# A transformer layer pair in float32 on one core: first selection, router, context keys and embedding products reordered at the start of the experts

## The chip, the cores and the metric

The kernel runs on one core of a Trainium2 chip. The metric is the device time of one execution, in microseconds (us). The runs shown have a median of 1193.95 us (three runs, 1192.86 to 1196.66). All data are float32.

## The reference, cut to what matters

Two blocks run one after the other on 256 tokens of width 1024. The first mixes (a gated linear recurrence and an attention), then adds a mixture of experts, then adds embeddings' rows times a gate. The second block (convolution, neighbourhood attention with context keys and values from `ctx_2`) follows.

```python
hm = rmsnorm(x, ln_moe[layer]).reshape(B * S, D)
x = x + hierarchical_moe(hm, ...)          # top-1 of 8 groups, then top-2 of its 8 experts
# per expert: (silu(x @ w1[e]) * (x @ w3[e])) @ w2[e], w1 and w3 1024x256, w2 256x1024
ple_gate = jax.nn.sigmoid(rmsnorm(x, ln_ple[layer]) @ w_ple_gate[layer])
x = x + (p[layer] @ w_ple_proj[layer]) * ple_gate
...
kv_c = hc @ w_in[i][:, K_OFF:V_END]        # context keys and values of the second block
```

Each of the 64 experts has three matrices of 1 MB, 192 in all, and every one of them is fetched from HBM.

## The kernel before, in words

All instructions stand in an order written out by hand, one stream for each engine, and engines meet on semaphores. TensorE (`pe`) multiplies, ScalarE (`act`) and VectorE (`dve`) empty its eight banks `B[0..7]`, and SyncE (`sp`) issues nearly all weight loads, in one order, each a DMA of 1 MB. A load for a place that is still in use waits on SyncE, and all later loads wait behind it.

**Stage A** ends with the product `out`, seven submatrix products (L820). Its result is `HN`, the residual. Then follow on TensorE, from L1071 to L1109: two of eight steps `k` of the context keys `kc` (one weight slot, two output halves `parts`, eight steps `k` each), the turning of `HN` (L1084), the other six steps of part 0 of `kc`, the router product (L1093, 8 steps `k` for each half of the tokens, operand `RHT`, which VectorE turns out at L1889 and ScalarE at L1358), part 1 of `kc`, five small products that rank the tokens within their group (L1100 to L1104, they need the group choice `GOH` of VectorE), and three of the four products `pp` of the embeddings (L802 here). `gather(0)` (L1121) needs the selection `SELR`, which VectorE computes in `select_chunk` (L2268). The fourth `pp` stands behind it. `moe_round(0)` follows.

VectorE's order there: logits (L2230), group choice (L2238 to L2245), the experts' logits in that group (L2248, L2250), choice of two experts (`first_max` twice, to L2254), then the rank (L2256 on), `select_chunk`, the tables, and only after the weights `WT` the `sorted_chunk(0)` (L2306), which writes the first gathered rows to `XGS`.

**The experts** run in rounds, one group of eight experts a round and up to 64 tokens; this input has eight rounds. In a round there are four pairs of experts `p`. `up(p)` (L1146) multiplies by `w1` and `w3` of both experts at once: one matmul has 64 stationary columns and streams 512 columns, 256 of `w1` and 256 of `w3`; the two experts use the two halves of the array's columns. `down(p)` (L1187) multiplies by `w2`. The order is up(0), up(1), down(0), up(2), down(1), [gather], up(3), down(2), down(3), then the scatter (L1225).

**Places for weights.** Round 0 has 24 loads. The first 20 have places of their own (`FIRST_PLACES`; B2, B1, B0, R0, VL, R1, R2, X, CK, R3 with two halves each), and are issued during stage A as memory comes free. R3 is the ring's last two slots: its half 0 holds `kc`'s weights before, its half 1 `w_ple_proj`'s. Every later load waits with `moe_used` until the earlier user of its place is done (`before`). A pair of loads of `up` counts as done together, when the whole of `up(p)` is done for that expert. The next loads are, in order: loads 20 to 23 of round 0 (places B2 and B1, free after up(0)); loads 0 to 3 of round 1 (B0 and R0, free after up(1)); loads 4 to 7 of round 1 (R1 and R2, free after up(2)); and so on. L687 issues a `w2`, L691 a `w1` or `w3`.

Of the kernel before, what the change touches and what calls it, by code (L numbers as in the profile page):

```python
# [21 lines left out]
P = 128  # L22
# [97 lines left out]
def build(nc, a, out):  # L120
    with ExitStack() as ctx:
# [113 lines left out]
        PTR = area(9728, 2, T)  # L235
# [15 lines left out]
        XGS = sb("XGS", [P, DK, T + SLOT])  # L251
        RS = sb("RS", [P, 16], I32)
# [185 lines left out]
        for i, n in zip(of["pp"], (0, 1, 3, 2)):  # L438
            bank_no[i] = n
# [108 lines left out]
        for _n in range(SET * UNITS):  # L548
            _r, _u = divmod(_n, UNITS)
            _down = moe_order[2 * _u][0] == "down"  # L550
            if _n < len(FIRST_PLACES):
                _p = FIRST_PLACES[_n]
            elif _r < BIG:
                _p = min((n, p) for p, (n, _) in last_use.items()
                         if (_down or p != "VL") and _n < GONE.get(p, SET * UNITS))[1]
            else:
                _p = RING_PLACES[_u % len(RING_PLACES)]
            past = last_use.get(_p)
            turn = past[1] + 1 if past else 1
            for _h in range(2):  # L560
                place_of[_r, 2 * _u + _h] = (_p, _h)
                turn_of[_r, 2 * _u + _h] = turn
                if past:
                    _q, _v = divmod(past[0], UNITS)
                    up = moe_order[2 * _v][0] == "up"
                    before[_r, 2 * _u + _h] = _q * NM + 2 * _v + (2 if up else 1 + _h)
            last_use[_p] = (_n, turn)
# [73 lines left out]
        def _(sp):  # L641
# [54 lines left out]
            for p, h in (("R0", 0), ("B1", 0), ("B0", 0), ("R0", 1), ("R1", 0), ("R1", 1), ("R2", 0), ("R2", 1), ("X", 0), ("X", 1),  # L696
                         ("CK", 0), ("CK", 1), ("R3", 0), ("VL", 1), ("R3", 1)):
# [14 lines left out]
            for j in range(2 * len(FIRST_PLACES), NM):  # L712
                sp.wait_ge(S("moe_used"), before[0, j])
                expert_dma(j, 0, 0)
# [11 lines left out]
            for r in range(1, SET):  # L726
                g = sp.value_load(RT[0:1, r + 1:r + 2], min_val=0, max_val=NG - 1)
                for j in range(NM):
                    sp.wait_ge(S("moe_used"), before[r, j])
                    expert_dma(j, r, g)  # L730
                    if (r, j) in ctx_behind:
# [37 lines left out]
        def _(pe):  # L769
# [317 lines left out]
            product(of["kc"][0], HT, parts=(0,), ks=range(2, DK))  # L1087
            pe.wait_ge(S("rT_dve"), 4)
            pe.wait_ge(S("rT_act"), 4)
            pe.wait_ge(S("small_in"), SMALL)  # L1090
            for t in range(TT):
                for k in range(DK):
                    mm = pe.matmul(B[4][:, t * 72:t * 72 + 72], RHT[:, k, t * P:t * P + P], RW[:, k, :],  # L1093
                                   start=(k == 0), stop=(k == DK - 1))
            mm.then_inc(S("logits_ps"), 1)
            product(of["kc"][0], HT, parts=(1,))
# [8 lines left out]
            pe.wait_ge(S("p_in"), 16)  # L1105
            for i in of["pp"][:-1]:
                product(i, PTR)


# [16 lines left out]
            def moe_round(r, first=False):  # L1126
# [3 lines left out]
                def up(p, halfway=None):  # L1130
# [4 lines left out]
                    js = [moe_index[("up", 2 * p + e, 0)] for e in range(2)]  # L1135
                    for j in js:
                        slot_in(j, r)
                        slot_in(j + 1, r)
                    for k in range(DK):
                        if k == DK // 2 and halfway is not None:  # L1140
                            turn_hidden(halfway)
                        for e in range(2):
                            pair = expert_pair(js[e], r)
                            w = pair.rearrange("p w (k n) -> p w k n", k=DK)[:, :, k, :]
                            xg = XGS[:, k, 0:SLOT] if first else XG[:, k, :]
                            mm = pe.matmul(bank[e * SLOT:e * SLOT + SLOT, :].rearrange("p (w n) -> p w n", w=2),  # L1146
                                           xg, w, start=(k == 0), stop=(k == DK - 1))
# [49 lines left out]
                if first:  # L1197
                    wait_emptied(of["pp"][3])
# [10 lines left out]
                for p in range(PAIRS):  # L1209
# [5 lines left out]
                    down(p, late=PAIRS - 1 if p + 2 == PAIRS else None)  # L1215
                    if isinstance(r, int) and (r, p) in CTX_AT:
# [12 lines left out]
            wait_emptied(of["pp"][0])  # L1229
            gather(0)  # L1230
            product(of["pp"][-1], PTR)
            wait_emptied(of["pp"][2])
# [113 lines left out]
        def _(act):  # L1346
# [192 lines left out]
            act.dma_start(PTR[:], a["pT"]).then_inc(S("p_in"), 16)  # L1539
# [17 lines left out]
            nc.scalar.activation(GEXP, GEXP, ACT.Exp).then_inc(S("moe_exp"), 1)  # L1557
            wait_result(act, of["kc"][0])
            context_keys(3, bank_of(of["kc"][0])).then_inc(S("emptied_act"), 1)
            act.wait_ge(S("moe_diff"), 2)  # L1560
            nc.scalar.activation(E2W, DLT, ACT.Exp).then_inc(S("moe_exp"), 1)
            embedding(0)
            for n in range(1, 4):
                embedding(n)

            def moe_round(r):
# [10 lines left out]
                for p in range(PAIRS):  # L1577
# [3 lines left out]
                    if p + 1 < PAIRS:  # L1581
                        sigmoid(p + 1)
                    if isinstance(r, int) and (r, p) in CTX_AT and p == 1:
# [274 lines left out]
        def _(dve):  # L1858
# [370 lines left out]
            for t in range(TT):  # L2229
                ins = V_.scalar_tensor_tensor(out=LGT[:, t, :], in0=B[4][:, 72 * t:72 * t + 72], scalar=rs["hm"][:, t:t + 1],  # L2230
# [20 lines left out]
            link(first_max(EL, M1, O1))  # L2251
            link(V_.scalar_tensor_tensor(out=EL2, in0=O1, scalar=-1e30, in1=EL, op0=ALU.mult, op1=ALU.add))
            link(first_max(EL2, M2, O2))
            V_.tensor_tensor(DLT, M2, M1, ALU.subtract).then_inc(S("moe_diff"), 1)  # L2254
# [17 lines left out]
            select_chunk()  # L2272
            link(V_.tensor_scalar(NR, CNT, 0.5, None, ALU.is_gt))
# [4 lines left out]
            link(V_.tensor_tensor(STA, ENDS, NR, ALU.subtract))  # L2278

# [22 lines left out]

            def sorted_chunk(n):

                dve.wait_ge(S("gath_ps"), n + 1)
                V_.tensor_tensor(XGS[:, :, n * SLOT:n * SLOT + SLOT], B[0][:, :].rearrange("p (k s) -> p k s", k=DK),  # L2306
                                 over(LNM[:].unsqueeze(2), DK, SLOT), ALU.mult).then_inc(S("xgs"), 1)
# [61 lines left out]
            sorted_chunk(0)  # L2369
# [266 lines left out]
```

## Time and profile before

| | |
|---|---|
| median of three runs | 1193.95 us (1192.86 to 1196.66) |
| the profiled execution | 1193.68 us |
| its span, first to last instruction | 1191.8 us |
| TensorE busy | 1129.6 us (95%) |
| VectorE, ScalarE, GpSimd busy | 507.4, 237.8, 115.1 us |
| moved by DMA | 325.82 MB, 273 GB/s over the span |
| granted TensorE clock, mean | 0.988 |

The profiled execution takes 1.9 us more than its span; that part lies around the instructions. A busy TensorE is not at its peak. The experts' rounds begin at 293 us and end at about 762 us. Times are measured from the span's start.

### The profile page before, as it was taken

To read this page: it belongs to the slowest core of one execution; us is meant where nothing else is said; L and a number is where in the kernel's file an instruction comes from. 1 tells how busy PE (TensorE), PEld (TensorE's weight loads), DVE (VectorE), ACT (ScalarE), POOL (GpSimd) and SP (SyncE) were. 2 spreads that over 40 slices of the span, in tenths; PEclk is the share of its full clock that TensorE was granted. 3 is DMA by queue.
4 is the path that set the end of the run, shared out by engine and by line. 5 is a ranking of instruction groups with operands and counts; after the bars stand their busy time and mean duration, and the time that the engine had idled before them with its cause. 6 is when DMAs were issued, how large, how long until landed. Compare 5 with 4: busy or idle time off the path is not lost.

```text
span 1191.8 us, 12664 instructions
## 1 busy us (share of the span) xinstructions
PE 1129.6 (95%) x4976; PEld 637.5 (53%) x4976; DVE 507.4 (43%) x862; ACT 237.8 (20%) x454; POOL 115.1 (10%) x116
## 2 busy tenths in 40 slices
PE   7999999999999998889999897899999999999995
PEld 6877888857434343434444242354448844457642
DVE  2246557475121211020202020475755666666576
ACT  2122664103000000000001010221001011058601
POOL 0016335000000000000000000000000030046300
PEclk9999999999999999999989999999999999999998
DMA  9999332658899999999999999954456454463310
GB/s 305 356 302 346 109 136 93 231 215 323 364 420 421 421 421 421 414 416 412 421 408 419 420 415 421 349 186 141 150 169 207 145 191 144 142 216 94 112 21 35
DMA packets 117628, 325.82 MB, mean 273 GB/s; under 512 B 9025, under 2 KB 62785, under 8 KB 92993
## 3 DMA queue, kind: packets, MB, share of 16 engines
q1 hardware_dynamic: 111752, 317.24, 70.6%
q0 software_dynamic: 1536, 4.20, 1.2%
q10 hardware_dynamic: 4280, 3.57, 0.9%
q8 instruction: 40, 0.66, 0.2%
q14 instruction: 20, 0.16, 0.0%
HBM read 322.89 MB, written 1.05 MB: 272 GB/s over the span
## 4 chain that ended last, share of the span: by engine, by line
PE 80%; DMA 10%; DVE 3%; ACT 2%; issue 2%; SPq 1%; POOL 1%; DVEq 0%; POOLq 0%; ACTq 0%
PE bank L820 23%; PE bank L799 16%; PE bank L1146 15%; PE bank L1187 7%; DMA ring<-in_w 6%; PE bank L802 5%; DMA AR<-in_w 4%; PE bank L1158 2%; PE bank L1309 1%; SPq L691 1%; PE bank L1121 1%; PE bank L1161 1%; PE bank L1329 1%; PE bank L1297 1%; PE bank L1225 1%
## 5 line engine op out<-in xcount | busy, mean ns | idle before, releaser
L799 PE MATMUL bank<-HT,ring 128*128 128x256 f32 x864 | 192.7, 380 | 0.0
L799 PEld LDWEIGHTS bank<-HT,ring 128*128 128x128 f32 x864 | 162.6, 190 | 27.8 <-issue 6.5
L1146 PE MATMUL bank<-ring,AR 128*64 128x512 f32 x480 | 147.3, 622 | 22.3 <-DMA AR<-in_w 13.4
L1146 PE MATMUL bank<-AR 128*64 128x512 f32 x416 | 130.2, 616 | 3.2 <-DMA AR<-in_w 3.0
L2330 DVE TENSOR_TENSOR AR<-AR,bank 128x256 f32<-128x256 f32 x32 | 13.5, 421 | 270.8 <-ACT AR L1572 270.4
L820 PE MATMUL bank<-ring,AR 128*128 128x512 f32 x280 | 122.1, 594 | 3.0 <-DVE AR L1889 1.8
L820 PE MATMUL bank<-ring,HN 128*128 128x512 f32 x224 | 97.3, 592 | 0.0
L1146 PEld LDWEIGHTS bank<-ring,AR 128*64 128x64 f32 x480 | 42.8, 142 | 96.8 <-issue 94.7
L820 PEld LDWEIGHTS bank<-ring,AR 128*128 128x128 f32 x280 | 52.5, 190 | 68.5 <-issue 66.9
L1755 POOL TENSOR_TENSOR SM<-SM 128x2 f32<-128x2 f32 (+3 forms) x8 | 11.6, 1448 | 676.1 <-DVE SM L1871 635.0
L820 PE MATMUL bank<-ring,HT 128*128 128x512 f32 x168 | 73.7, 592 | 0.0
L820 PEld LDWEIGHTS bank<-ring,HN 128*128 128x128 f32 x224 | 42.6, 190 | 53.6 <-issue 53.6
L2352 DVE TENSOR_TENSOR HN<-HN,bank 128x512 f32<-128x512 f32 x32 | 31.2, 1042 | 84.4 <-PE bank L1225 84.4
L1146 PEld LDWEIGHTS bank<-AR 128*64 128x64 f32 x416 | 38.3, 141 | 50.5 <-issue 49.7
L1187 PE MATMUL bank<-ring,AR 128*64 128x512 f32 x288 | 65.1, 594 | 0.0
L1579 ACT ACTIVATE AR<-bank 128x256 f32<-128x256 f32 x32 | 12.3, 384 | 203.8 <-PE bank L1173 203.8
L820 PEld LDWEIGHTS bank<-ring,HT 128*128 128x128 f32 x168 | 31.7, 190 | 38.3 <-issue 38.0
L1187 PE MATMUL bank<-AR 128*64 128x512 f32 x192 | 44.1, 594 | 0.0
L1187 PEld LDWEIGHTS bank<-ring,AR 128*64 128x64 f32 x288 | 20.2, 137 | 38.9 <-issue 35.9
L1572 ACT ACTIVATE AR<-bank 128x256 f32<-128x256 f32 x32 | 12.3, 384 | 141.8 <-PE bank L1146 141.8
L802 PE MATMUL bank<-ring,AR 128*128 128x256 f32 (+1 forms) x136 | 30.8, 388 | 7.4 <-DMA ring<-in_w_in 7.2
L1920 DVE TENSOR_TENSOR ring<-ring 128x2048 f32<-128x2048 f32 x12 | 27.5, 2292 | 23.6 <-PE bank L820 23.6
(388 smaller groups left out, 1399.6 us busy)
## 6 DMA issues: line engine op xcount, KB each, us to landing
ring<-in_w SPq DMA_DIRECT2D x104, 1024.0 KB, 19.1
AR<-in_w SPq DMA_DIRECT2D x84, 1024.0 KB, 16.2
ring<-in_w_in SPq DMA_DIRECT2D x60, 1024.0 KB, 7.0
ring<-in_w_mod SPq DMA_DIRECT2D x12, 1024.0 KB, 10.5
AR<-in_w_in SPq DMA_DIRECT2D x6, 1024.0 KB, 21.3
ring<-in_w_out SPq DMA_DIRECT2D x4, 1024.0 KB, 5.1
LATE<-in_w SPq DMA_DIRECT2D x4, 1024.0 KB, 21.2
ring<-in_w_ple_gate SPq DMA_DIRECT2D x4, 1024.0 KB, 10.7
```

The lines of the kernel that those rows point to most:

```text
L691: sp.dma_start(dst.rearrange("p (k n) -> p k n", k=DK), src).then_inc(there, 16)
L799: mm = pe.matmul(bank[:, part * T:part * T + T], w[:, k, c0 + part * P:c0 + part * P + P], act[:, k, :], start=(k == 0), stop=(k == k_n - 1))
L802: mm = pe.matmul(bank[:, part * 256:part * 256 + n], act[:, k, part * P:part * P + P], w[:, k, c0:c0 + n], start=(k == 0), stop=(k == k_n ...
L820: mm = pe.matmul(bank[:, :], stationary(k), slot_view(f)[:, k, :], start=(k == 0), stop=(k == 3))
L1146: mm = pe.matmul(bank[e * SLOT:e * SLOT + SLOT, :].rearrange("p (w n) -> p w n", w=2), xg, w, start=(k == 0), stop=(k == DK - 1))
L1158: mm = pe.matmul(bank[:, part * T:part * T + T], w[:, k, part * P:part * P + P], HT[:, k, :], start=(k == 0), stop=(k == DK - 1))
L1187: mm = pe.matmul(B[5][half * SLOT:half * SLOT + SLOT, :], HHT[:, p % 2, c, e * SLOT:e * SLOT + SLOT], w[:, c, half * 512:half * 512 + 512] ...
L1572: nc.scalar.activation(SGM[:, p % 2], B[3 + p % 2][:, 0:FE], ACT.Sigmoid).then_inc(S("moe_sig"), 1)
L1579: nc.scalar.activation(HHT[:, p % 2].rearrange("p c s -> p (c s)"), B[6 + p % 2][:, 0:2 * P], ACT.Copy)\
L1920: V_.tensor_tensor(w22, w22, w11, ALU.subtract).then_inc(S("seven_dve"), 1)
L2330: V_.tensor_tensor(SGM[:, p % 2], SGM[:, p % 2], bank[:, 0:FE], ALU.mult).then_inc(S("moe_dve"), 1)
L2352: ins = V_.tensor_tensor(hn, hn, B[SCATTER[2 * t + half]][:, :].rearrange("p (q k) -> p q k", k=DK), ALU.add)
```

## The change

The diff is shown without its context lines where these only repeat the function's frame.

* The router's eight steps are taken in the order of arrival of `RHT`'s columns (0, 4, 1, 5, ...), each behind its own wait, into bank 3 and no longer bank 4.
* `kc` is cut into pieces around the router: part 0 steps 2 to 5 ahead of it; steps 6 and 7 and part 1's step 0 behind it; steps 1 to 4 behind the rank products; steps 5 to 7 behind `gather(0)`.
* VectorE does rank and `select_chunk` before the choice of two experts, and `sorted_chunk(0)` right behind the round counts.
* `up(0)` of round 0 multiplies by `w1` of both experts first, then by `w3`, in matmuls that stream 256 columns, and counts `moe_used` after each half; loads 20 and 22 may start after the first half, 21 and 23 after the second.
* The four embedding products stand behind `down(0)` of round 0; their operand `PTR` lies in `XGS`; ScalarE's copies (`embedding`) follow in its round.
* On SyncE, `R3`'s half 1, whose slot holds `w_ple_proj`, is loaded behind load 3 of round 1, once the embedding products are done.

```diff
@@ -232,7 +232,6 @@
         PP = area(6144, TT, D)
-        PTR = area(9728, 2, T)
         CSQ = area(M0 + 6720, TT, D)
@@ -249,6 +248,7 @@
         XGS = sb("XGS", [P, DK, T + SLOT])
+        PTR = XGS[:, 1:5, SLOT:SLOT + P]
         RS = sb("RS", [P, 16], I32)
@@ -435,7 +435,7 @@
-        for i, n in zip(of["pp"], (0, 1, 3, 2)):
+        for i, n in zip(of["pp"], (0, 2, 1, 0)):
             bank_no[i] = n
@@ -564,6 +564,9 @@
                     before[_r, 2 * _u + _h] = _q * NM + 2 * _v + (2 if up else 1 + _h)
+                    if _q == 0 and _v < 2:
...
+                        before[_r, 2 * _u + _h] = 2 * _h + _v + 1
             last_use[_p] = (_n, turn)
@@ -694,7 +697,7 @@
             for p, h in (("R0", 0), ("B1", 0), ("B0", 0), ("R0", 1), ("R1", 0), ("R1", 1), ("R2", 0), ("R2", 1), ("X", 0), ("X", 1),
-                         ("CK", 0), ("CK", 1), ("R3", 0), ("VL", 1), ("R3", 1)):
+                         ("CK", 0), ("CK", 1), ("VL", 1), ("R3", 0)):
                 if p[0] == "R":
@@ -709,7 +712,7 @@
                 expert_dma(first(p, h), 0, 0)
-            for j in range(2 * len(FIRST_PLACES), NM):
+            for j in sorted(range(2 * len(FIRST_PLACES), NM), key=lambda j: before[0, j]):
                 sp.wait_ge(S("moe_used"), before[0, j])
@@ -728,6 +731,9 @@
                     expert_dma(j, r, g)
+                    if (r, j) == (1, 3):
+                        sp.wait_ge(S("res_a"), last_result[NA - 1] + 1)
+                        expert_dma(first("R3", 1), 0, 0)
                     if (r, j) in ctx_behind:
@@ -1084,16 +1090,18 @@
                         mm.then_inc(S("turned"), 1)
-            product(of["kc"][0], HT, parts=(0,), ks=range(2, DK))
-            pe.wait_ge(S("rT_dve"), 4)
-            pe.wait_ge(S("rT_act"), 4)
+            product(of["kc"][0], HT, parts=(0,), ks=range(2, 6))
             pe.wait_ge(S("small_in"), SMALL)
+            by_arrival = [k for pair in zip(range(4), range(4, 8)) for k in pair]
             for t in range(TT):
-                for k in range(DK):
-                    mm = pe.matmul(B[4][:, t * 72:t * 72 + 72], RHT[:, k, t * P:t * P + P], RW[:, k, :],
-                                   start=(k == 0), stop=(k == DK - 1))
+                for k in by_arrival:
+                    if t == 0:
+                        pe.wait_ge(S("rT_dve" if k < 4 else "rT_act"), k % 4 + 1)
+                    mm = pe.matmul(B[3][:, t * 72:t * 72 + 72], RHT[:, k, t * P:t * P + P], RW[:, k, :],
+                                   start=(k == by_arrival[0]), stop=(k == by_arrival[-1]))
             mm.then_inc(S("logits_ps"), 1)
-            product(of["kc"][0], HT, parts=(1,))
+            product(of["kc"][0], HT, parts=(0,), ks=range(6, DK))
+            product(of["kc"][0], HT, parts=(1,), ks=range(1))
@@ -1102,10 +1110,21 @@
             pe.matmul(B[5][:, 16:24], ONE, GOH[:, 1, :], start=False, stop=True).then_inc(S("rank_ps"), 1)
-            pe.wait_ge(S("p_in"), 16)
-            for i in of["pp"][:-1]:
-                product(i, PTR)
...
+            product(of["kc"][0], HT, parts=(1,), ks=range(1, 5))
...
+            def embedding_products():
...
+                pe.wait_ge(S("p_in"), 16)
+                for i in of["pp"]:
+                    _, f, c0, _, n = results[i]
+                    wait_bank(i)
+                    if c0 == 0:
+                        wait_slot(pe, f)
+                    for part in range(TT):
+                        for k in range(2):
+                            mm = pe.matmul(bank_of(i)[:, part * n:part * n + n], PTR[:, 2 * k + part, :],
+                                           slot_view(f)[:, k, c0:c0 + n], start=(k == 0), stop=(k == 1))
+                    mm.then_inc(S("res_a"), 1)
@@ -1133,6 +1152,20 @@
                     js = [moe_index[("up", 2 * p + e, 0)] for e in range(2)]
+                    xg = XGS[:, :, 0:SLOT] if first else XG
+                    if first and p == 0:
...
+                        for half in range(2):
+                            for j in js:
+                                slot_in(j + half, r)
+                            for k in range(DK):
+                                for e in range(2):
+                                    w = expert_weights(js[e] + half, r, DK)[:, k, :]
+                                    mm = pe.matmul(bank[e * SLOT:e * SLOT + SLOT, half * FE:half * FE + FE],
+                                                   xg[:, k, :], w, start=(k == 0), stop=(k == DK - 1))
+                                    if k == DK - 1:
+                                        mm.then_inc(S("moe_used"), 1)
+                        return
                     for j in js:
@@ -1142,9 +1175,8 @@
                             w = pair.rearrange("p w (k n) -> p w k n", k=DK)[:, :, k, :]
-                            xg = XGS[:, k, 0:SLOT] if first else XG[:, k, :]
                             mm = pe.matmul(bank[e * SLOT:e * SLOT + SLOT, :].rearrange("p (w n) -> p w n", w=2),
-                                           xg, w, start=(k == 0), stop=(k == DK - 1))
+                                           xg[:, k, :], w, start=(k == 0), stop=(k == DK - 1))
                             if k == DK - 1:
@@ -1195,7 +1227,7 @@
                 if first:
-                    wait_emptied(of["pp"][3])
+                    wait_emptied(of["kc"][0])
                 pe.wait_ge(S("sel"), at(1, 1))
@@ -1213,6 +1245,8 @@
                     down(p, late=PAIRS - 1 if p + 2 == PAIRS else None)
+                    if first and p == 0:
+                        embedding_products()
                     if isinstance(r, int) and (r, p) in CTX_AT:
@@ -1226,10 +1260,8 @@
-            wait_emptied(of["pp"][0])
             gather(0)
-            product(of["pp"][-1], PTR)
-            wait_emptied(of["pp"][2])
+            product(of["kc"][0], HT, parts=(1,), ks=range(5, DK))
             moe_round(0, first=True)
@@ -1536,7 +1568,7 @@
             act.wait_ge(S("merged"), 4)
-            act.dma_start(PTR[:], a["pT"]).then_inc(S("p_in"), 16)
+            act.dma_start(PTR, a["pT"].rearrange("p k (t q) -> p (k t) q", t=TT)).then_inc(S("p_in"), 16)
@@ -1555,13 +1587,10 @@
             nc.scalar.activation(GEXP, GEXP, ACT.Exp).then_inc(S("moe_exp"), 1)
+            act.wait_ge(S("moe_diff"), 2)
+            nc.scalar.activation(E2W, DLT, ACT.Exp).then_inc(S("moe_exp"), 1)
             wait_result(act, of["kc"][0])
             context_keys(3, bank_of(of["kc"][0])).then_inc(S("emptied_act"), 1)
-            act.wait_ge(S("moe_diff"), 2)
-            nc.scalar.activation(E2W, DLT, ACT.Exp).then_inc(S("moe_exp"), 1)
-            embedding(0)
-            for n in range(1, 4):
-                embedding(n)
@@ -1580,6 +1609,9 @@
                         sigmoid(p + 1)
+                    if isinstance(r, int) and (r, p) == (0, 0):
+                        for n in range(4):
+                            embedding(n)
                     if isinstance(r, int) and (r, p) in CTX_AT and p == 1:
@@ -2227,7 +2259,7 @@
             for t in range(TT):
-                ins = V_.scalar_tensor_tensor(out=LGT[:, t, :], in0=B[4][:, 72 * t:72 * t + 72], scalar=rs["hm"][:, t:t + 1],
+                ins = V_.scalar_tensor_tensor(out=LGT[:, t, :], in0=B[3][:, 72 * t:72 * t + 72], scalar=rs["hm"][:, t:t + 1],
                                               in1=RB[:], op0=ALU.mult, op1=ALU.add)
@@ -2248,10 +2280,6 @@
                 link(V_.tensor_reduce(EL[:, t, :], GEX.rearrange("p g e -> p e g"), AX_X, ALU.add))
-            link(first_max(EL, M1, O1))
-            link(V_.scalar_tensor_tensor(out=EL2, in0=O1, scalar=-1e30, in1=EL, op0=ALU.mult, op1=ALU.add))
-            link(first_max(EL2, M2, O2))
-            V_.tensor_tensor(DLT, M2, M1, ALU.subtract).then_inc(S("moe_diff"), 1)
             dve.wait_ge(S("rank_ps"), 1)
@@ -2270,12 +2298,24 @@
+            def sorted_chunk(n):
...
+                dve.wait_ge(S("gath_ps"), n + 1)
+                V_.tensor_tensor(XGS[:, :, n * SLOT:n * SLOT + SLOT], B[0][:, :].rearrange("p (k s) -> p k s", k=DK),
+                                 over(LNM[:].unsqueeze(2), DK, SLOT), ALU.mult).then_inc(S("xgs"), 1)
...
+            link(first_max(EL, M1, O1))
+            link(V_.scalar_tensor_tensor(out=EL2, in0=O1, scalar=-1e30, in1=EL, op0=ALU.mult, op1=ALU.add))
+            link(first_max(EL2, M2, O2))
+            V_.tensor_tensor(DLT, M2, M1, ALU.subtract).then_inc(S("moe_diff"), 1)
             link(V_.tensor_scalar(NR, CNT, 0.5, None, ALU.is_gt))
...
             link(V_.tensor_tensor(STA, ENDS, NR, ALU.subtract))
+            sorted_chunk(0)
@@ -2299,12 +2339,6 @@
-            def sorted_chunk(n):
...
-                dve.wait_ge(S("gath_ps"), n + 1)
-                V_.tensor_tensor(XGS[:, :, n * SLOT:n * SLOT + SLOT], B[0][:, :].rearrange("p (k s) -> p k s", k=DK),
-                                 over(LNM[:].unsqueeze(2), DK, SLOT), ALU.mult).then_inc(S("xgs"), 1)
@@ -2366,7 +2400,6 @@
             V_.tensor_tensor(WT, O1, O2, ALU.add).then_inc(S("moe_x"), 1)
-            sorted_chunk(0)
```

## Rows read from the trace of the kernel before

**Rows 1.** The page, by 40 equal slices: GB/s that the DMA engines moved.

```profile
GB/s 305 356 302 346 109 136 93 231 215 323 364 420 421 421 421 421 414 416 412 421 408 419 420 415 421 349 186 141 150 169 207 145 191 144 142 216 94 112 21 35
```

**Rows 2.** The chain that ended last, experts' rounds: start us, us, what.

```profile
456.02 27.27 DMA ring<-in_w
...
721.21 20.20 DMA ring<-in_w
```

**Rows 3.** Busy time by stretch: stretch, its us, engines' busy us (x), clock, DMA share, GB/s.

```profile
292.00:294.00 2.00, 2.00 (x11) 1.16 (x11) 1.76 (x9) 0.62 (x2) 0.00 (x0) 1.00 0.00 0
...
298.00:300.00 2.00, 2.00 (x12) 0.57 (x8) 0.00 (x0) 0.00 (x0) 0.00 (x0) 1.00 0.00 0
...
305.00:490.00 185.00, 176.09 (x843) 66.80 (x844) 31.05 (x67) 13.93 (x35) 0.00 (x0) 0.99 1.01 421
```

**Rows 4.** SyncE's DMA issues in order of time: start us, us, line, destination, count.

```profile
281.76 0.33 SPq L691 DMA_DIRECT2D ring<-in_w  x1
...
293.36 0.33 SPq L691 DMA_DIRECT2D ring<-in_w  x1
...
300.37 3.16 SPq L687 DMA_DIRECT2D AR<-in_w  x4
308.85 0.83 SPq L691 DMA_DIRECT2D AR<-in_w  x2
...
319.72 1.81 SPq L691 DMA_DIRECT2D ring<-in_w  x4
...
449.59 8.51 SPq L691 DMA_DIRECT2D ring<-in_w  x4
```

**Rows 5.** Single issues at 293.36, 300.37, 319.72 us: last number, us to landing.

```profile
ring<-in_w SPq DMA_DIRECT2D x1, 1024.0 KB, 4.7
...
AR<-in_w SPq DMA_DIRECT2D x1, 1024.0 KB, 5.8
...
ring<-in_w SPq DMA_DIRECT2D x1, 1024.0 KB, 6.3
```

**Rows 6.** The chain that ended last, 274 to 316 us.

```profile
274.44 3.79 PE bank L1093 x32
278.23 3.50 PE bank L799 x16
...
282.74 5.28 PE bank L802 x24
288.03 3.52 PE bank L1121 x32
...
293.33 7.02 PE bank L1146 x32
...
312.10 3.43 PE bank L1146 x16
```

**Rows 7.** Instructions of VectorE in order of time: start us, us, then as above.

```profile
272.72 1.66 DVE L1889 TENSOR_SCALAR AR<-bank,LNM 128x256 f32<-128x256 f32 x4
278.27 0.49 DVE L2230 SCALAR_TENSOR_TENSOR AR<-bank,SM,RB 128x72 f32<-128x72 f32 x2 [3.89 <-PE bank L1093]
...
279.71 0.17 DVE L2245 TENSOR_TENSOR SM<-AR,SM 128x16 f32<-128x16 f32 x1
...
280.65 0.27 DVE L2250 TENSOR_REDUCE SM<-AR 128x8 f32<-128x64 f32 x1
...
283.31 0.17 DVE L2256 COPY SM<-bank 128x16 f32<-128x16 f32 x1
...
284.63 0.54 DVE L2268 TENSOR_SCALAR SELR<-CST,SM 128x64 f32<-128x64 f32 x2
...
291.58 0.69 DVE L2306 TENSOR_TENSOR XGS<-bank,LNM 128x512 f32<-128x512 f32 x1 [1.00 <-PE bank L1121]
```

**Rows 8.** TensorE's weight loads in order of time: start us, us, idle before.

```profile
278.00 3.33 PEld L799 LDWEIGHTS bank<-HT,ring 128*128 128x128 f32 x16
...
293.74 0.14 PEld L1146 LDWEIGHTS bank<-AR,XGS 128*64 128x64 f32 x2 [0.28 <-issue]
```

## The prediction

> **What bounds the kernel now.** I read the page's slices first, then the chain of waits, then stretches of 2 us around the start of the experts, then SyncE's issues. The slices [rows 1] show 420 or 421 GB/s from the twelfth slice (328 us) on, and nothing near it before and after the experts: their loads run at a flat ceiling for over 400 us. The chain agrees. In the late rounds it passes through waits for weights of 20 to 27 us [rows 2], though a load that meets an empty queue lands 4.7 us after its issue [rows 5]. The rest is time in the queue, and the queue is full: four issues take 8.51 us of SyncE's time there [rows 4], about 2.1 us each, where a free queue takes 0.4. So from about 305 us [rows 3] to the end of the experts the end is set by one sum: the moment at which the unbroken stream begins, plus all bytes that then remain. One load of 1.049 MB at 421 GB/s is 2.49 us. What TensorE does meanwhile changes nothing, unless it frees a place so late that the stream breaks.
>
> Before 305 us the stream is broken. It moves nothing in 292 to 294 us and in 298 to 300 us [rows 3]. The issues [rows 4] say why: SyncE waits for places. One load goes at 281.76 (`kc` done), one at 293.36 (the last embedding product done), four at 300.37 (up(0) done), four from 308.85 (up(1) done), four at 319.72 (up(2) done). Since 300.37 the stream has held, but barely. The eight loads of 300.37 and 308.85 take 8 x 2.49 = 19.9 us. The load issued at 319.72 lands 6.3 us later, a lone one 4.7 us after its issue and the first of a group of four 5.8 us [rows 5]. So it waited only 0.5 to 1.6 us in the queue. Call this cover c; it is the pivot of the whole argument.
>
> TensorE, on the other hand, has no gap of note between 274.44 and the start of up(0) at 293.33 [rows 6]: waits for selection and rank are hidden under `kc` and embedding products.
>
> **The change part by part.** The sum is made against the profiled execution: span 1191.8 us, 1193.68 us with 1.9 us around it. The median of the runs is 1193.95 us, 0.3 us higher.
>
> *Router.* `kc` piece ahead of it: two of six steps less. Part 1 has eight steps in 3.50 us [rows 6], 0.44 us each, so the router may begin 0.88 us earlier than 274.44, at about 273.5. VectorE's four columns of `RHT` end in steps of 0.4 us from about 273.1 to 274.4 [rows 7]; by order of arrival the last one is seventh, needed at 273.5 + 6 x 0.24 = 274.9. So it runs through: 3.79 us, end 277.3 in place of 278.23. I take 0.9 us gained; bounds 0 (the eight waits hold it up as before) and 1.1.
>
> *Group and rank.* From logits (278.27) to the first instruction behind the group choice (279.71) are 1.44 us [rows 7]; so group at 278.8. TensorE fills 277.3 to 278.6 with three steps of `kc` (1.31 us) and waits 0.2 us. Five rank products take 282.74 - 281.73 = 1.01 us (from 278.23 + 3.50) [rows 6]: until 279.8. Then four steps of `kc`, 1.75 us: until 281.6.
>
> *Selection.* VectorE's expert logits end 1.21 us after group (279.71 to 280.92 [rows 7]), here at 280.0, with the rank ready. From the rank copy to the end of `SELR` are 285.17 - 283.31 = 1.86 us [rows 7]: 281.9, in place of 285.17. TensorE waits 0.4 us. Gather 3.52 us: 285.5; three steps of `kc`, 1.31 us: 286.8. `sorted_chunk(0)`, 0.69 us, is done at 286.3, hidden under them. up(0) starts at 286.8 in place of 293.33, 6.5 us earlier. But four embedding products, 4 x 5.28/3 = 7.04 us, have only been moved behind `down(0)`. Net, TensorE has lost d = 0.5 us (both new waits, less what the router gained). The choice of two experts and the tables, moved behind the selection on VectorE, end before the weights `WT` are wanted at the end of up(0), since everything on VectorE but that choice moves up together; cost 0. If that cover is gone, each us goes into d.
>
> *up(0) in two halves.* 64 matmuls of 256 columns in place of 32 of 512: the same columns, double the weight loads. A pair now takes 7.02/16 = 0.44 us and its two loads, side by side, 0.14 us, with 0.28 us idle before them [rows 8]. Half as long, 0.22 us, still covers 0.14. The 128 x 128 loads of L799 are hidden under matmuls of the same 0.22 us (16 loads in 3.33 us [rows 8], no idle between). I take 0.3 us for 64 more instructions; bounds 0 and 16 x 2 x 0.14 = 4.5 us (nothing hidden).
>
> The Trainium skill speaks against this edit: "TensorE: Matmul & The Clock Gate", section "Part 3: Packing small matmuls", says that a weight load overlaps with matmuls in flight only where the row groups differ, and here all 128 rows are used. By that rule the load would stand in the open already, and up(0) would pay for the added ones: a rival below. The row speaks otherwise: 0.44 us a pair for 512 columns is twice the 0.22 us that L799 takes for 256, with nothing added for the loads.
>
> *Transfers.* First half of up(0) done at 290.4: loads 20 and 22; second at 294.1: loads 21 and 23. Load of R3 half 0 goes at 286.8 (before 281.76), VL half 1 at 279.8. up(1) ends 6.2 us earlier (6.5 less 0.3), and its four loads go at 302.6 in place of 308.85. down(0), which ends at 312.10 before [rows 6], ends at 305.9 by the same shift, the embedding products at 312.9, and then R3 half 1 goes, which before went at 293.36. It lands at about 318 and is wanted by up(3) at about 328: covered by 10 us. SyncE stands at this wait until 312.9, but the loads behind it (R1, R2) come free only with up(2), so nobody waits for that.
>
> *What this is worth.* up(2) ends where it did plus d: 0.5 + 0.3 = 0.8 us, so 320.5 us. By then nine loads are through: the last lands at 318, and the stream now breaks from about 316 to 322 us. The stop of 292 to 302 us is filled, and a new one opened ahead of the same gate. The same bytes remain behind the same gate, R1's first load, issued at 320.5. It lands there 4.7 to 5.8 us later, before 319.72 + 6.3 = 326.0. So the end moves by d - c = 0.8 - (0.5 to 1.6) = -0.8 to +0.3 us. I take -0.2 us: 1193.68 - 0.2 = 1193.5 us.
>
> **The rivals.**
> *A, the early start carries through.* First loads of the round start 290.4 and not 300.37. If the stream held from there, the end would come up to 9.9 us earlier, 1183.8 us; if half of it, 1188.7 us. For it: the empty stretches [rows 3] are real. Against: only nine loads, 22.4 us, can be had before up(2) ends, and 292.4 + 22.4 = 314.8. It needs up(2) some 5 us earlier, and TensorE had no idle time to give.
>
> *B, the halves of up(0) pay for their weight loads (slower).* Place: the 64 matmuls. If the period of a pair exceeds 0.28 us, d grows by 32 x 0.06 = 2 us and more; at full price d = 0.5 + 4.5 = 5.0 and the end moves by 5.0 - 1.0 = +4.0 us: 1197.7 us. It decides against the forecast from d = c, 1 us, and shows as slower from d = 4.6. For it: the rule named above. Against: L799 [rows 8].
>
> *C, selection does not come early.* If VectorE or the waits in the router hold `SELR` back to near 285, TensorE idles, with the embedding products no longer there: d up to 285.17 - 281.6 = 3.6 us in place of 0.4, the end +2.7 + 0.8 - 0.5, about 1196.7 us. Against: every step of VectorE's chain has its row.
>
> *D, restart.* After an empty queue a group of four may come into stride slower than the first landing shows: +1 us, 1194.7 us. It lies within the forecast's range.
>
> **How the numbers follow.** A change under 0.3%, 3.6 us, can hardly be told from none by a measurement of this kernel. The forecast with D (1191.5 to 1195.5) has 0.78, A 0.10, B 0.07, C 0.05. A is over the bound in most of its range: faster 0.10. B at full price, a little of C and what I have not seen: slower 0.09. Same 0.81. The range reaches to the near part of A and to B's price: 1189.5 to 1197.7 us.
>
> **What would show it.** Right: up(0) (L1146's line) starts near 287 us, its 64 matmuls take about 7.3 us; `SELR` ends near 282; the embedding products stand at 306 to 313 us; DMA is busy from 295 and empty for some 5 us before 322 us; R1's first load is issued at 320 to 321 us and from there everything lies as before, moved by under 1 us. Wrong: no empty stretch ahead of up(2)'s end, up(2) ending before 318 us, or later rounds in which the stream breaks. If the time falls by over 4 us, the view that the remaining bytes behind up(2)'s gate set the end has failed.

## The result, and the profile after

The changed kernel takes 1196.34 us (median of 8 runs, 1195.05 to 1200.15), the kernel before 1193.26 us beside it: ratio 1.0024, interval 1.0015 to 1.0032. It is slower by 3.1 us; forecast was 1193.5. A second series (f1) gave 1195.30 against 1193.61: 1.0014, 1.0005 to 1.0023. So the loss is 1.7 us in one series and 3.1 in the other.

The chain of the changed kernel, start of the experts (start us, us, what), answers to [rows 6]:

```profile
273.25 3.70 PE bank L1100 x32
...
281.86 3.79 PE bank L1140 x32
285.64 1.35 PE bank L805 x6
287.00 7.06 PE bank L1164 x64
...
305.81 7.10 PE bank L1125 x32
...
320.51 3.43 PE bank L1219 x16
```

Router from 273.25, gather at 281.86, up(0) at 287.0 and 7.06 us long in its 64 matmuls, embedding products at 305.8, up(2)'s end at 320.5: forecast were 273.5, 281.9, 286.8, 7.3, 305.9 and 320.5. SyncE's issues answer to [rows 4]:

```profile
287.03 0.33 SPq L694 DMA_DIRECT2D ring<-in_w  x1
290.62 4.26 SPq L690 DMA_DIRECT2D AR<-in_w  x4
302.55 0.83 SPq L694 DMA_DIRECT2D AR<-in_w  x2
303.58 19.77 SPq L694 DMA_DIRECT2D ring<-in_w  x7
```

And stretches of 2 us (last number GB/s) answer to [rows 3]: the stop of 292 to 300 us is gone, a new one stands at 318 us, ahead of the load that up(2) frees.

```profile
316.00:318.00 2.00, 2.00 (x12) 0.80 (x10) 0.00 (x0) 0.38 (x1) 0.00 (x0) 1.00 0.56 225
318.00:320.00 2.00, 2.00 (x12) 0.66 (x10) 0.00 (x0) 0.00 (x0) 0.00 (x0) 1.00 0.00 0
320.00:322.00 2.00, 2.00 (x12) 0.63 (x10) 0.91 (x2) 0.38 (x1) 0.00 (x0) 1.00 0.51 74
...
330.00:450.00 120.00, 117.91 (x570) 44.56 (x568) 24.86 (x52) 9.75 (x24) 0.00 (x0) 1.00 1.01 422
```

So far the trace is the forecast's. What it had not: the last wait of the experts and the work behind it. The chain of the kernel before, behind its last transfer of the experts [rows 2], and then that of the changed one:

```profile
741.54 3.65 PE bank L1146 x16
```

```profile
722.64 20.35 DMA ring<-in_w
...
743.12 5.29 PE bank L1178 x16
```

The last wait ends 1.6 us later, and the same 16 matmuls take 1.6 us more. Stretches of the changed kernel (the third number from the end is the granted clock) show why:

```profile
742.00:744.00 2.00, 0.88 (x3) 0.33 (x4) 0.00 (x0) 0.00 (x0) 0.00 (x0) 0.76 1.02 426
744.00:746.00 2.00, 2.00 (x8) 0.81 (x6) 0.00 (x0) 0.00 (x0) 0.00 (x0) 0.50 1.01 422
```

The clock is at its lower level, 1.2 GHz, just where TensorE's work is on the path, behind a wait of 2.2 us without matmuls. All 3.2 us of the longer span (1195.0 against 1191.8) are in these two numbers. From the end of the last wait to the end of the span are 450.3 us in the kernel before, 451.9 here.

### The profile page after: what moved, and what is told of

It reads as the page before. It is cut to its first block, busy times and chain, and to the rows that moved or that the text cites. A ratio compares the mean times of both kernels' runs of the same rounds, so it can differ in the third digit from the quotient of the medians.

```text
span 1195.0 us, 12728 instructions
## 1 busy us (share of the span) xinstructions
PE 1132.0 (95%) x5008; PEld 640.0 (54%) x5008; DVE 507.8 (42%) x862; ACT 237.8 (20%) x454; POOL 114.0 (10%) x116
## 4 chain that ended last, share of the span: by engine, by line
PE 80%; DMA 10%; DVE 3%; SPq 2%; ACT 2%; issue 1%; POOL 1%; DVEq 0%; POOLq 0%; ACTq 0%
PE bank L826 23%; PE bank L805 16%; PE bank L1178 14%; PE bank L1219 6%; DMA ring<-in_w 6%; PE bank L808 4%; DMA AR<-in_w 4%; PE bank L1190 2%; SPq L694 1%; PE bank L1341 1%; PE bank L1140 1%; PE bank L1193 1%; PE bank L1361 1%; PE bank L1329 1%; PE bank L1259 1%
## 5 line engine op out<-in xcount | busy, mean ns | idle before, releaser
L808 PE MATMUL bank<-ring,HT 128*128 128x256 f32 x160 | 35.8, 381 | 0.0
```

Of the source, the lines that this page charges most:

```text
L808: mm = pe.matmul(bank[:, part * 256:part * 256 + n], act[:, k, part * P:part * P + P], w[:, k, c0:c0 + n], start=(k == 0), stop=(k == k_n ...
```

## The experiments

Each ran beside the kernel before. The medians are of all executions of a run; "wait" and "tail" are of its one trace and split that trace's span: "wait" is where the row after the last transfer of the experts starts in the chain, "tail" the span less that.

| run | median us | before us | ratio, interval | wait | tail |
|---|---|---|---|---|---|
| before | 1193.26 | | | 741.54 | 450.3 |
| changed | 1196.34 | 1193.26 | 1.0024, 1.0015 to 1.0032 | 743.12 | 451.9 |
| e1 up(0) whole | 1194.27 | 1193.96 | 1.0003, 0.9994 to 1.0012 | 741.46 | 450.2 |
| e2 products behind up(2) | 1194.01 | 1193.96 | 0.9997, 0.9988 to 1.0005 | 740.49 | 452.0 |
| e3 two products twice | 1197.87 | 1193.96 | 1.0029, 1.0018 to 1.0040 | 745.23 | 450.3 |
| e4 products ahead of up(0) | 1195.22 | 1193.96 | 1.0013, 1.0004 to 1.0022 | 741.61 | 451.9 |
| f1 changed, again | 1195.30 | 1193.61 | 1.0014, 1.0005 to 1.0023 | 742.84 | 451.9 |
| f2 halves, late loads | 1196.28 | 1193.61 | 1.0019, 1.0010 to 1.0029 | 742.30 | 452.2 |
| f3 R3 behind load 5 | 1191.82 | 1193.61 | 0.9987, 0.9978 to 0.9996 | 739.04 | 450.4 |
| f4 f3, up(0) whole | 1193.49 | 1193.61 | 0.9994, 0.9985 to 1.0004 | 739.18 | 452.5 |
| g1 before +0.88 | 1195.03 | 1193.88 | 1.0010, 1.0001 to 1.0019 | 741.19 | 452.0 |
| g2 before +1.76 | 1196.69 | 1193.88 | 1.0022, 1.0013 to 1.0031 | 743.13 | 452.0 |
| g3 changed -0.88 | 1193.04 | 1193.88 | 0.9997, 0.9988 to 1.0006 | 741.00 | 450.3 |
| g4 R3 behind load 6 | 1192.23 | 1193.88 | 0.9990, 0.9979 to 1.0000 | 738.42 | 452.0 |
| h1, h3 changed (one run each) | 1194.63, 1195.93 | 1193.19 | | 742.51, 741.55 | 450.3, 452.6 |
| h2, h4 before (one run each) | 1193.41, 1193.61 | 1193.19 | | 741.26, 741.49 | 450.3, 450.3 |

In eight of the 18 traces the tail is 450.2 to 450.4 us, and the granted clock is nowhere down behind the last wait. In the other ten it is 451.9 to 452.6 us, and in each of them a stretch behind the last wait, between 740 and 770 us, has the lower clock; below this is called a drop in the tail.

**e1.** In the expert branch of `up`, and with `before` as in the kernel before:

```diff
-                    if first and p == 0:
+                    if False:
```

> The changed kernel with one edit undone: up(0) of round 0 streams w1 and w3 together again (32 matmuls of 512 columns), and loads 20 to 23 wait for its end. Theory (gate): the end is set by the moment at which up(2) of round 0 frees R1 and R2; up(0) took 7.06 us in halves and 7.02 us whole, so that gate stays at 320.7 us, the stream of loads still runs empty ahead of it, and the time stays within 0.6 us of the changed kernel's 1196.3. Rival (halves cost): the 32 added weight loads or the two early issues disturb something; the time returns to 1193.3 us.

1194.27 us, on the rival's side. But the gate did not move (R1's first load is issued at 320.40 us, against 320.68), nor did the 7.0 us of up(0); the last wait ends at 741.46 and no drop follows. This is no verdict on the halves: with the halves kept, g3 below is as fast, and f3 is faster than f4, which has up(0) whole.

**e3**, the size of the gate:

```diff
-                    for part in range(TT):
+                    for part in [*range(TT)] * (2 if c0 in (0, 256) else 1):
```

> The changed kernel in which two of the four embedding products are computed twice (same values), 3.55 us more of TensorE ahead of up(2). Theory (gate): up(2) ends at 324.2 us, the stream starts anew that much later, and the end moves by 3.55 us: 1199.9 us, give or take 0.8 for drops of the clock. Rival (the later waits of TensorE for weights, some 15 to 20 us a round, take the added work up): 1196.3 us, no change.

The time, 1197.87 us, is a miss, 1.2 us under the expected 1199.1 to 1200.7. Against the two series of the changed kernel the median rises by 1.5 and 2.6 us. The gate opens at 324.04 us, 3.5 later than the 320.54 of h3, a further trace of the changed kernel with the same pace of issues behind the gate; the stream of loads lies 3.4 us later at the same byte from 200 MB on, and the last wait ends 3.7 us later. So later waits take none of it up, and the rival is out. What keeps the median down is behind that: this trace has no drop in its tail, and the changed kernel often has one.

**e4** (`embedding_products()` between `kc`'s last piece and `moe_round(0)`, its copies and R3's load moved with it).

> The changed kernel with the embedding products back ahead of up(0), behind gather(0) and kc, and R3's half 1 loaded when they are done, ahead of loads 20 to 23. up(2)'s end stays at 320.7 us, but the four first loads go at about 297.7 and 301.2 us, so the queue is empty for only about a us ahead of the gate and not for five. Theory (gate with a cost of the restart): the gate is the same, but the stream restarts from a short break: 1195.3 to 1196.3 us. Rival (the restart from empty costs nothing; the gate alone counts): 1196.3 us. Rival (the transfers' early start is worth something): slower than the changed kernel, 1197 us or more.

1195.22 us, just under the theory's range. The wait ends at 741.61, as in the kernel before; the trace has a drop in the tail (451.9). How long the queue was empty ahead of the gate hardly counts.

**e2**, the gate moved on purpose:

```diff
+                    if first and p == 1:
+                        embedding_products()
                     down(p, late=PAIRS - 1 if p + 2 == PAIRS else None)
-                    if first and p == 0:
-                        embedding_products()
...
-                    if (r, j) == (1, 3):
+                    if (r, j) == (1, 7):
```

> The changed kernel with the four embedding products (7.1 us of TensorE) behind up(2) and not ahead of it; R3's half 1 is loaded behind load 7 of round 1. Theory (gate): R1 and R2 come free 7.1 us earlier, at 313.6 us; the eight loads ahead of them, issued from 290.6 and 302.5 us, last until about 315, so the stream holds from 303 us, and the end comes earlier until the next gate, the end of up(3) at about 336.5 us, which binds 4 us earlier than before: 4 to 7 us off 1196.3, 1189 to 1192 us. Rival (TensorE's total work sets the end): the same work in another order, 1196 us.

Against the changed kernel it is faster by 1.3 to 2.3 us, against the kernel before it is no gain, and 1194.01 us misses the expected 1189 to 1192. The trace tells why (TensorE in order of time, then stretches of the same kernel):

```profile
328.45 1.08 PE L1178 MATMUL bank<-AR,XGS 128*64 128x512 f32 x1 [2.06 <-DMA ring<-in_w]
```

```profile
326.00:328.00 2.00, 0.39 (x4) 0.25 (x3) 0.00 (x0) 0.00 (x0) 0.00 (x0) 0.88 0.98 410
328.00:330.00 2.00, 1.55 (x4) 0.59 (x6) 0.00 (x0) 0.00 (x0) 0.00 (x0) 0.50 1.04 434
```

up(3) waits 2.06 us for R3's half 1, the clock falls to 1.2 GHz, its matmuls take 1.06 in place of 0.59 us, and the next gate (CK, R3) opens at 339.2 us and not at 336. A short wait in round 0 cost more by the clock than by itself: 14 matmuls take until 334.41 us, 3.0 us longer than at the full clock.

**f3**, R3's half 1 issued earlier:

```diff
-                    if (r, j) == (1, 7):
+                    if (r, j) == (1, 5):
```

> As the run with the embedding products behind up(2), but R3's half 1 is loaded behind load 5 of round 1 and not behind load 7. There up(3) waited 2.06 us for R3's half 1, and a drop of the clock to one half for 6.8 us followed, so that the gate of CK and R3 opened at 339.2 and not at 336. Theory (gates): R3's half 1 now lands about 324 us, ahead of up(3) at 326.5; no wait, no drop; CK and R3 come free at about 335.3 us, while the queue still has work until 338: no break of the stream from 303 us on, and the whole stream lies 5 to 6 us earlier than in the kernel before. Time 1188 to 1189.5 us. Rival (something else binds in the later rounds, and a gain in the stream is given back): 1192 us or more, as before.

1191.82 us, faster than both kernels. No wait of up(3), wait's end 739.04, 2.5 us ahead of the kernel before; 5 to 6 were expected. The missing part is a break that I had overlooked, in SyncE's wait for the embedding products with nothing queued (stretch of f3):

```profile
320.00:322.00 2.00, 2.00 (x11) 0.74 (x11) 0.00 (x0) 0.60 (x1) 0.00 (x0) 1.00 0.29 37
```

**f4**, f3 with up(0) whole, and **g4**, `(1, 6)` in place of `(1, 5)`.

> The run with R3's half 1 behind load 5 and the embedding products behind up(2), but with up(0) of round 0 whole and loads 20 to 23 behind its end. Theory (gates): with the stream unbroken from 303 us on, the early loads now count: they start at 293 and 294 us in place of 289.4 and 292.8, the eight loads from there end 2 to 3 us later, and so does the whole stream: 1190.5 to 1191.5 us, 2 to 3 us above the run with halves. Rival (halves are worth nothing or cost as they did in the changed kernel): same or faster than the run with halves.

> As the run with R3's half 1 behind load 5, but behind load 6. There SyncE waited for the embedding products until 320.4 us with the queue empty from about 320.6, so that R3's half 1 landed 4.5 us behind load 5 where 2.5 is the pace: a break of 2 us. With load 6 ahead the queue has work until 323; R3's half 1 lands about 325.5 us, ahead of up(3) at 327.7. Theory (gates): the stream gains 2 us, 340.5 in place of 342.5 us at 90 MB; time 1189.8 us. Rival: the next gate (CK and R3 at 335.6 us) binds at once and gives it back: 1191.8 us. A wait of up(3) would show as a drop of the clock and cost more.

f4's last wait ends at 739.18, f3's at 739.04: with the stream bound by the break at 320 us the early loads are worth nothing, and the halves cost nothing. Its median is 1.7 us higher, with a tail of 452.5. g4 closes the break, the wait ends at 738.42, 0.6 us ahead of f3's, though its stream of loads lies 1.9 us ahead of f3's from 200 MB on (the 16 parts of the load it waits for land over 4.4 us, f3's over 3.4). The tail has a drop, and the runs spread from 1189.71 to 1196.62; 1192.23 misses the expected 1189.8, and g4 is not shown to be better than f3.

**f1 and f2.** f1 is the changed kernel; f2 has

```diff
-                        before[_r, 2 * _u + _h] = 2 * _h + _v + 1
+                        before[_r, 2 * _u + _h] = 3 + _v
```

> The changed kernel itself, unaltered, for a second trace and more times beside the kernel before. Theory: of the 3.2 us by which its first profiled span was longer, 0.76 us lie in the stream of loads from 82 MB on and come again in every run, and the rest (a later last receipt of a load, and one drop of the clock at 743 us while TensorE works on the last pair of matrices) depends on where the drops fall: the new trace shows 0.5 to 1 us in the stream, and 0 to 2.5 us behind it. The median stays 1.5 to 3 us above the kernel before. Rival: the whole 3 us is a fixed cost of the program; the new trace shows the same drop at 743 us and the same split.

> The changed kernel with up(0) still in two halves, but loads 20 to 23 all issued only when the second half is done, in the order 20, 21, 22, 23. With up(0) whole the time was 0.3 us above the kernel before, with it in halves about 3. Theory 1 (the early issues matter): time as with up(0) whole, 1194.3 us. Theory 2 (the 64 matmuls matter, by a gate 0.3 us later and SyncE's slow second issue behind it): 1195.5 to 1196.5 us, and load 5 of round 1 is issued 0.4 to 1.2 us behind load 4 by the trace.

f1: its stream of loads is 0.1 us behind that of the kernel before, where 0.5 to 1 us was expected, and the drop stands at another place. Its 16 matmuls behind the wait take 3.65 us, and the granted clock has a mean of 0.89 from 754 to 770 us (chain, then the stretch); tail 451.9 as well.

```profile
742.84 3.65 PE bank L1178 x16
```

```profile
754.00:770.00 16.00, 11.53 (x49) 5.07 (x46) 7.80 (x13) 4.24 (x9) 0.69 (x1) 0.89 1.05 377
```

f2: 1196.28, as the changed kernel in its first series; the early issues are not the cause.

**g1, g2, g3**: no new instruction of the change, only time ahead of the gate. g1 and g2 repeat half of the last embedding product in the kernel before, once and twice; g3 leaves the second step out of one embedding product of the changed kernel.

```diff
+            for _ in range(1):
+                product(of["pp"][-1], PTR, parts=(0,))
             product(of["pp"][-1], PTR)
```

> The kernel before with half of its last embedding product computed twice (four matmuls, 0.88 us of TensorE ahead of up(0); same values). Theory 1 (place and clock): what the changed kernel lost is its gate about 0.9 us later, worth 0.3 to 0.7 us in the stream, and beyond that more frequent drops of the clock in the last waits, which come from where these waits lie in time; so this kernel loses 1 to 2.5 us as well: 1194.8 to 1196 us beside 1193.7. Theory 2 (the change's new instructions themselves, such as up(0) in halves): only the stream's 0.3 to 0.7 us are lost, 1194 to 1194.4 us.

> The kernel before with 1.76 us of TensorE more ahead of up(0) (half of the last embedding product computed three times). The first loads of the round and up(2)'s end both move by 1.76 us, so the stream, which holds from the first of them, moves by 1.7 us (the cover of the queue helps only where later gates move and the first does not): stream +1.7 us. Theory 1 (place and clock): time +1.7 plus or minus 1 us, not in step with the +0.88 run. Theory 2: in step, +1.7 us: 1195.4 us.

> The changed kernel with 0.88 us less of TensorE ahead of up(2): one of the four embedding products leaves out its second step k (its values lack that half). The gate falls back to where it was in the kernel before. Theory 1 (place and clock): stream 0.2 to 0.9 us earlier than in the changed kernel, and the median falls back by 1 to 3 us, to 1193 to 1194.5. Theory 2 (the new instructions): the stream gains up to 0.9 us, the rest of the loss stays: 1194.8 to 1195.5 us.

g3: with 0.88 us less work the median, 1.7 and 3.1 us above the kernel before for the changed kernel, is 0.8 below it. g1: 0.88 us more in the kernel before costs 1.15 us, though its last wait even ends 0.35 us early; its tail has the drop (452.0) that the three traces of the kernel before have not. That trace doesn't show a later place, though: its work up to `kc` ended 1.1 us earlier (the load behind it is issued at 280.68 us, against 281.76 [rows 4]), which is more than the 0.88 us added. g2: 2.8 us for 1.76 us of work, wait 1.6 later, and a drop. All edits of the change are in g3, less four matmuls, and none is in g1 and g2: a loss comes without the change's instructions and goes with them in place. That fits the place in time as the cause, and there is no sign of a fixed cost of the new instructions.

**h1 to h4**, single runs for their traces.

> The changed kernel, a third trace. Theory 1 (place and clock): stream within 0 to 0.8 us of the kernel before at the same byte; a drop of the clock between 740 and 770 us, where TensorE's work is on the path, as in both traces so far. Rival: no drop there, and the loss lies elsewhere.

> The kernel before, a second trace. Theory 1: no drop of the clock between 740 and 770 us in most traces, as in the first. Rival: such a drop is as frequent as in the changed kernel.

> The changed kernel, a fourth trace. Theory 1: again a drop between 740 and 770 us and a stream 0 to 0.8 us later. Rival: no such drop.

> The kernel before, a third trace. Theory 1: no drop of the clock between 740 and 770 us. Rival: such a drop, and a span over 1193 us with it.

With the first traces: a drop in the tail in three of four traces of the changed kernel, in none of three of the kernel before. h1 (chain, 742.51) has none, and its span is 1192.8 us; h3 has one between 764 and 768 us, behind the idle time in which the last rows are added up:

```profile
764.00:768.00 4.00, 2.68 (x3) 1.17 (x4) 3.31 (x8) 2.04 (x6) 0.70 (x1) 0.50 1.07 374
```

Its last wait ends at 741.55, as before, yet its span is 1194.1 us.

Three or four traces are few, but every execution, traced or not, has a span and a mean granted clock on record. All ten traces with a drop in the tail have a mean of 0.987 or less, and seven of the eight without one have 0.988 or more (e1's has 0.986: the mean counts drops anywhere). Of the changed kernel's 21 executions 13 have 0.987 or less, of the kernel before's 99 with a clock on record 45, so that one has drops too, and the two shares are not clearly apart. In g1 and g2 it is 20 of 22, against 13 of 33 of the kernel before beside them: there the difference is clear. And among executions with 0.988 or more the changed kernel's mean span is 1193.0 us, the other's 1191.8: 1.2 us are lost without the clock.

## Why the prediction was wrong, point by point

*What bounds the kernel* (the unbroken stream behind up(2)'s gate): right. e3 moves gate and end together, e4 leaves both, f3 gains by an earlier gate.

*Router, rank, selection, gather*: each within 0.4 us. Router 3.70 us without a stop; `SELR` ended at 281.8.

*up(0) in halves*: 0.04 us in place of 0.3; its rival B is out, as no added time shows there. The Trainium skill, "TensorE: Matmul & The Clock Gate", section "Part 3: Packing small matmuls", has weight loads overlap only where row groups differ. This trace differs: 32 more loads on all rows, 7.06 us against 7.02 [rows 6].

*d*: forecast 0.8 us. The gate opened at 320.68 against 319.72 [rows 4], 0.96; in h3 0.82, in f1 0.70. In h1, where all work ahead of the experts ran 1.2 us earlier, it is -0.21.

*Rival A*: out; the stop was filled and a new one opened, as the sum had it. *Rival C*: out; `SELR` came early and TensorE had no idle time to give up.

*The step that failed* is "the end moves by d - c = -0.8 to +0.3", which held everything behind the gate to be rigid and put the clock at nothing, without a reason. The forecast was -0.2 us. In its place the traces show three terms, given here as means of four traces of the changed kernel less means of three of the kernel before.

First, +0.4 us by which the stream came later, at the same byte. Gate and stream are in us later than in the first trace of the kernel before (319.72 us; the stream by ten points from 200 to 245 MB); the cover is the difference:

| trace | gate | SyncE's 2nd issue behind it, us | stream | cover | load of the last wait lands over, us |
|---|---|---|---|---|---|
| changed | +0.96 | 1.23 | +0.77 | 0.19 | 4.5 |
| f1 | +0.70 | 1.08 | +0.13 | 0.57 | 4.7 |
| h1 | -0.21 | 1.37 | +0.19 | -0.40 | 4.3 |
| h3 | +0.82 | 0.38 | +0.04 | 0.78 | 3.3 |
| e1 | +0.68 | 0.38 | -0.09 | 0.77 | 3.4 |
| e3 | +4.32 | 0.38 | +3.47 | 0.85 | 3.6 |
| e4 | +0.80 | 0.38 | -0.03 | 0.83 | 3.8 |
| g3 | +0.08 | 0.38 | -0.72 | 0.80 | 3.7 |
| f2 | +0.81 | 1.44 | +0.39 | 0.42 | 3.7 |

The cover c was real: 0.8 us, within the 0.5 to 1.6 of the forecast, in five traces that agree within 0.1 us. It was lost, in part or wholly, in the four in which SyncE's second issue behind the gate took over 1 us (0.38 in all three traces of the kernel before). That is rival D, the slow restart, in another form: it cost 0.2 to 1.2 us in three of four traces of the changed kernel. Why that issue takes longer, the runs do not show.

Secondly, +0.6 us by which the load of the last wait is complete later than the stream's bytes say. The trace has 16 landings for each load, and the wait ends with the last of them. In the kernel before they lie 3.5 to 3.7 us apart, first to last, in the changed kernel 3.3 to 4.7. This and the stream make the 1.1 us by which the last wait ends later (742.51 against 741.43). Whether the change widens it, or these four traces happen to, stays open.

Thirdly, +1.35 us in the tail: 450.3 us without a drop of the clock, 1.6 to 2.3 us more with one, and the changed kernel had one in three of four traces. The prediction has no term for it. [Rows 3] gave a mean clock of 0.99 for a stretch full of waits, and I never asked whether a wait stands ahead of work on the path. The sum is 0.4 + 0.6 + 1.35 = 2.4 us, between the 1.7 and 3.1 us of the two series. The section "HAM oscillation" of the same page of the Trainium skill describes waits for data of 3 to 5 us that leave the clock down for the work behind them. Here a wait of 2.2 us did so (5.29 us in place of 3.65), and one of 2.1 us in f1 did not: the trace shows the effect, at a shorter wait and not each time. It should have been a rival.

That 1196.34 us lies within the stated range is luck: its upper end is B's price, and B did not happen. Two slips of the working change nothing: D's 1194.7 us is 1193.5 + 1, so 1194.5; and the slices of the experts hold 408 to 421 GB/s [rows 1], not 420 or 421.

That a drop in the tail lengthens it is shown by the 18 tails. That the place in time makes a drop more or less frequent is shown for the kernel before with more work (g1 and g2, by their executions' clocks); for the changed kernel it rests on the medians of one run, g3, and the start of the experts itself lies up to 1.2 us apart in traces of one program (h1 against the first). By what rule a given wait loses the clock stays open.

## What to carry to other kernels

Where loads queue without a stop from a gate on, filling an earlier stop was worth nothing here: find the gate, and move work from ahead of it to behind it (f3, -1.8 us), instead of within what lies ahead. Work moved past a load's wait must leave the queue something to do meanwhile. And in a kernel that waits for weights, look at every wait ahead of work on the path: what TensorE's clock does behind it was worth more here than the change. One trace of each kernel would have hidden this: compare several, and the clocks of the executions without one.

## What the runs showed of the hardware that was not expected

A wait of 2.06 us in e2 was followed by matmuls at 1.06 in place of 0.59 us, while waits of 2.2 us in the kernel before (until 741.5 us) and 2.1 us in f1 (until 742.8 us) were followed by matmuls at full pace. A load that meets an empty queue lands 4.8 us after issue (f3, the load issued at 320.55 us), as the 4.7 us of [rows 5]; the loads of a full one end 2.5 us apart. The 16 parts of a load that met an empty queue land within 0.3 us (f3, landed at 325.3 us), those of a load after 400 us of full queue over 3.3 to 4.7 us, and neighbouring loads of a trace have the same spread within 0.1 us. So the end of the wait follows the slowest part, about 1 us later in some traces than in others with the same bytes moved. The same program's median moved between two series of runs by 1.0 us, with the kernel before unchanged to 0.4 us.
